# Moving projection pieces so that products on the divided array stand side by side, in a gated DeltaNet and sliding-window attention layer

## The reference

```
h    = rmsnorm(x, pre_norm_w)
proj = h @ w_in                    # q, k, v, gate za (4 heads x 128); b, a (4 + 4); qb, kb, vb, gate zb
# group A: gated DeltaNet
qkv  = silu(causal_depthwise_conv(q, k, v))          # 4 taps
beta = sigmoid(b); g = -exp(a_log) * softplus(a + dt_bias); G = cumsum(g) in a chunk
lower = strict_lower((beta k) k^T * decay)           # 64 x 64 in each chunk
value, k_cum = (I + lower)^-1 [beta v, beta k exp(G)]
o_a  = chunk recurrence over a 128 x 128 state per head
o_a  = rmsnorm(o_a, dn_out_norm_w) * silu(za)
# group B: 8 query heads, 2 key/value heads of 64, a window of two chunks, one sink per head
p    = softmax([rope(qb) rope(kb)^T / 8, sink]) without the sink's column
o_b  = (p vb) * silu(zb)
out  = x + rmsnorm([o_a, o_b] @ w_out, post_norm_w)
```

## Time and profile before

| | |
|---|---|
| median of three runs | 2222.03 us (2221.86 to 2222.96) |
| profiled execution | 2220.89 us, span 2219.1 us |
| one steady step (scores at 1000.99 and 1066.05) | 65.1 us |
| TensorE busy | 94% of the span |
| VectorE / ScalarE / GpSimd busy | 75% / 35% / 31% |
| mean granted TensorE clock | 0.991 of full |
| chain that ended last | TensorE 82%, VectorE 13%, ScalarE 2% |
| DMA | 34 GB/s on average |

### The profile page before, as it was taken

How to read it: one execution, slowest core, us unless ns; L and a number is a source line. 1 busy time by engine, 2 the same in 40 slices (tenths; PEclk the granted TensorE clock), 3 DMA queues, 4 the chain that set the end, 5 groups by cost and what they waited for, 6 DMA issues and landing times.

```text
span 2219.1 us, 63767 instructions
## 1 busy us (share of the span) xinstructions
PE 2089.9 (94%) x26854; PEld 1700.3 (77%) x26854; DVE 1655.8 (75%) x4880; ACT 772.4 (35%) x2200; POOL 688.4 (31%) x1035
## 2 busy tenths in 40 slices
PE   0389999999999999999999999999999999999996
PEld 0378778878878877887887788788788778878874
DVE  5887777777777777777777777777777777777773
ACT  0533333333333333333333333333333333333332
POOL 0023333332323333332333323233322323332332
PEclk9999999999999999999999999999999999999997
DMA  7101000010000100000000000001100000001000
GB/s 296 65 22 32 2 31 32 32 31 32 31 2 31 32 31 32 32 29 4 31 32 31 31 31 17 17 32 32 32 31 31 6 27 32 32 31 32 22 2 29
DMA packets 26335, 75.37 MB, mean 34 GB/s; under 512 B 5129, under 2 KB 9538, under 8 KB 25026
## 3 DMA queue, kind: packets, MB, share of 16 engines
q1 hardware_dynamic: 26050, 71.29, 9.4%
HBM read 54.50 MB, written 16.78 MB: 32 GB/s over the span
## 4 chain that ended last, share of the span: by engine, by line
PE 82%; DVE 13%; ACT 2%; issue 1%; DMA 1%; SPq 0%; POOL 0%; POOLq 0%; DVEq 0%; ACTq 0%
PE bank L406 31%; PE bank L608 15%; PE bank L413 12%; PE bank L421 9%; DVE qkv L896 4%; PE bank L461 2%; PE bank L438 2%; PE bank L576 2%; PE bank L443 1%; PE bank L543 1%; DVE qkv L894 1%; PE bank L564 1%; DVE w_raw L1242 1%; PE bank L384 1%; DVE small L935 1%
## 5 line engine op out<-in xcount | busy, mean ns | idle before, releaser
L406 PE MATMUL bank<-xt_half,w_raw 128*128 128x128 f16 x15360 | 933.0, 219 | 54.5 <-DVE w_raw L1242 53.9
L406 PEld LDWEIGHTS bank<-xt_half,w_raw 128*128 128x128 f16 x15360 | 890.8, 98 | 66.9 <-DVE w_raw L1242 54.1
L896 DVE SCALAR_TENSOR_TENSOR qkv<-conv_in,cols,qkv 128x128 f32<-128x128 f32 x1152 | 436.4, 421 | 3.5
L413 PE MATMUL bank<-w_raw,xt_half 128*128 128x264 f16 (+1 forms) x1536 | 283.7, 328 | 1.0
L1301 POOL TENSOR_TENSOR cw<-mt,small 128x128 f32<-128x128 f32 x320 | 135.1, 446 | 344.7 <-PE bank L438 321.1
L413 PEld LDWEIGHTS bank<-w_raw,xt_half 128*128 128x128 f16 x1536 | 144.3, 99 | 84.3 <-DVE w_raw L911 8.3
L715 ACT ACTIVATE work<-bank 128x128 f32<-128x128 f32 x160 | 44.4, 277 | 372.3 <-PE bank L443 372.3
L608 PE MATMUL bank<-w_o,inv_t 128*128 128x512 f16 x768 | 171.0, 379 | 2.1 <-DVE inv_t L1175 2.1
L608 PE MATMUL bank<-w_o,out_b_half 128*128 128x512 f16 x768 | 171.0, 379 | 0.0
L675 ACT ACTIVATE tanh_c<-qkv 128x512 f32<-128x512 f32 x96 | 60.5, 630 | 281.5 <-DVE qkv L896 281.5
L1349 POOL TENSOR_TENSOR small<-small 128x1 f32<-128x1 f32 x32 | 6.2, 193 | 435.2 <-ACT work L815 435.2
(11 more groups left out here) (215 smaller groups left out, 3575.4 us busy)
## 6 DMA issues: line engine op xcount, KB each, us to landing
x_in<-in_x_dram SPq DMA_DIRECT2D x32, 512.0 KB, 4.7
y_out<-in_x_dram SPq DMA_DIRECT2D x32, 512.0 KB, 4.0
out_dram<-y_out SPq DMA_DIRECT2D x32, 512.0 KB, 2.9
w_raw<-in_w_in_dram SPq DMA_DIRECT2D x8, 1024.0 KB, 13.5
w_o<-in_w_out_dram SPq DMA_DIRECT2D x8, 512.0 KB, 13.4
w_raw<-in_w_in_dram SPq DMA_DIRECT2D x8, 384.0 KB, 12.4
w_raw<-in_w_in_dram SPq DMA_DIRECT2D x8, 256.0 KB, 13.2
rot_tab<-in_rotary_dram SPq DMA_DIRECT2D x32, 64.0 KB, 4.2
```

The costliest lines, as they stand in the source:

```text
L406: last = mm(dst[:, 128 * b:128 * b + 128], w_half[:, c, ws, col:col + 128], xt_half[:, xs, c, :], start=(c == 0 and ws + xs == 0), stop=(c ...
L413: last = mm(dst[:, 0:n_col], xt_half[:, xs, c, :], w_half[:, c, ws, col:col + n_col], start=(c == 0 and ws + xs == 0), stop=(c == NC - 1 a ...
L896: last = v.scalar_tensor_tensor(dst, conv_in[:, b, i:i + TOK], tap, dst, ALU.mult, ALU.add)
```

## The change

Five edits in the step, four on TensorE and one on VectorE:

```diff
                 done(pe, k_win_ready, m)
                 done(pe, at_ready, m)
-                fill(1)
+                fill(2)
...
                 last.then_inc(scores_ready, 1)
-                fill(1)
                 level_p(1)
                 fill(1)
                 level_t(1)
...
                 level_p(3)
+                fill(1)
 
                 done(pe, soft_ready, m)
                 for hh in range(8):
                     last = nc.tensor.transpose(heads(4 + hh // 4)[:, hh % 4, :], soft[:, hh, :], ident)
                 last.then_inc(soft_turned, 1)
                 fill(1)
-                level_t(3)
-                fill(1)
-
                 done(pe, soft_t_ready, m)
                 done(pe, v_win_ready, m)
+                level_t(3)
                 for kv in range(2):
...
+                    couple(1)
                     for half in range(2):
                         last = v.tensor_reduce(row_max[:, 4 * half:4 * half + 4], heads(4 + half), AX_X, ALU.max)
                     last.then_inc(soft_link, 1)
-                    couple(1)
                     dve.wait_ge(soft_link, m * 5 + 1)
```

## The result

The changed kernel takes 2259.99 us (median of four runs, 2258.18 to 2261.03) against 2221.95 for the kernel before (2221.66 to 2222.96). The ratio is 1.017, 95% interval 1.0152 to 1.0187: 38 us slower, where 35 were forecast. The profiled execution took 2258.18 us with a span of 2256.4, 37.3 above the span before.

A forecast was written before the change was run, and what follows sets the result against it. TensorE, busy 94% of the span, was taken as the bound. Per step, waits of 1.23 and 0.29 less 0.41 saved make 1.11 us; 31 steps give 34.4, plus 0.5 for the last: 2257 us, range 2246 to 2270.

The forecast's parts named there:

- The first wait: At the first key/value/gates piece (L413), moved ahead of the scores: TensorE waits 1.23 us a step for VectorE's gate product.
- The second wait: At level 2's first product (L438): TensorE waits 0.29 us a step for VectorE's level update, behind mask and softmax work.
- The reason given for 0.28 instead of 0.48: VectorE's L1066 to L1071 takes 0.28 us, since GpSimd, released by the same product, is done during the reductions.
- The savings: Tiling switches taken away at the scores and around level 3 and the value products: 0.41 us less a step.
- its 0.21: Cost in us of leaving the scores for the next piece, part of it the wait for the gate product L911.
- The seam between the two kinds of tiles: Between level 3's 64*64 product and the 128*64 value products: costs 0.09 us, as much as one to the full array.
- The last step: The mix step without pieces gains at level 1, loses at level 3 waiting for ScalarE's copies; 0.5 us charged.
- Only the first wait: Rival: VectorE gets through the softmax work 0.3 us sooner; 0.82 us a step, 2248 us; chance 0.10.
- hidden: Rival: the gate product comes in time for the moved piece, so not slower; 2218 or 2209 us; chance 0.03.
- the clock falls: Rival: each new wait lowers TensorE's granted clock, 53 us more, 2310 us; chance 0.07.
- More waits: Rival: probabilities' copies and the slower 0.48 add up to 0.4 us a step, to 2269 us; beyond 2264 chance 0.10.
- The wait at L468: At level 6's product, TensorE's 0.3 us wait for VectorE, 31 times: shifts along and gives nothing back.

The follow-up runs named there:

- e1: The changed kernel with the tanh of the gate columns za moved ahead of level 0's four copies on ScalarE; 2221.59 us.
- e3: The changed kernel with the tanh of za ahead of level 0's copies and level 1's mask back behind the two row-maximum reductions; 2212.14 us.
- e5: The kernel before with only the tanh of za moved ahead of level 0's copies on ScalarE; 2219.49 us.
- e4: The kernel before with only the level 3 part: one more piece ahead of the probabilities' transposes, level 3's second product next to the value products; 2220.32 us.

## Why the prediction was right

- *The first wait.* Forecast 1.23, measured 1.23; e1 removes it and it alone. The cause was as read: the kvb piece shares a bank with za, and za's reader starts only behind ScalarE's copies.
- *The second wait.* Forecast 0.29, measured 0.39. Its chain on VectorE was right (mask to L984 3.41 us in the trace, counted from the start of the mask to the end of the update; the sum had 1008.30 - 1004.91 = 3.39). What was mis-sized is when level 2's product is due: level 1's first product, behind the scores, takes 0.23 to its transposes instead of 0.28, so TensorE came 0.05 sooner and waited that much longer for a VectorE that did not come sooner. This half costs the step nothing, as it is also saved ahead of the wait. The other 0.05 does, and is nearly all by which the step outgrew the forecast (1.17 against 1.11): from the start of the first kvb piece to level 2's product it is 1024.24 - 1017.96 = 6.28, forecast 1008.35 - 1002.12 = 6.23. It is made up of links of 0.01 to 0.02 (start of the mask 2.81 behind the piece against 2.79, the 3.41, and 0.06 against 0.05 to TensorE).
- *The reason given for 0.28 instead of 0.48* from L1066 to L1071, that GpSimd would be done by then, fits: 0.28 was measured in the changed kernel, with GpSimd's work of that time over. No run separates GpSimd from whatever else lay beside these two instructions.
- *The savings.* Forecast 0.41. In the changed kernel they are 1.23 + 0.39 - 1.17 = 0.45, with the 0.05 of the shorter first product. Measured as the step of e3 against before, they are 0.40, with 0.08 of waits left in it (0.02 at level 1, 0.06 at level 2). As the forecast said of its 0.21 without giving a size, a part of this is no switch: 0.10 is the old wait for the gate product (e5), so the switches are worth 0.10 + 0.11 + 0.10 = 0.31. The seam between the two kinds of tiles stays, as forecast; e4 shows 0.10 for that part and not 0.2.
- *The sum.* Little of its closeness is luck: of the 0.10 by which the second wait is off, 0.05 is matched by 0.05 more saved, as said. 31 x 1.166 = 36.1 us, and 1.1 us besides, make the 37.3 us of the two spans. The 1.1 are 0.3 ahead of the first mixed step, 0.4 more than 1.17 in that step, 0.2 less in the last step with pieces and 0.6 in the one without. The forecast had 34.4 and 0.5. The median moved by 38.0.
- *The last step.* Of the effects named, both came: level 1's second product waits 0.53 us in place of 1.62, and level 3's second product waits 1.18 us for ScalarE's copies there. A third was not foreseen there: level 2's product waits 2.72 us in place of 1.39, since level 1 is ready early and the update stands behind the reductions.
- *The rivals.* "Only the first wait" is refuted by the 0.39, "hidden" by the 31 waits at L413 (that wait is hidden only where the tanh is moved, e1), "the clock falls" by the window with 1.00. "More waits" did not come in the changed kernel; the transposed probabilities were in time, by 0.15 us (the copies end at 1032.53, the product starts at 1032.68).
- *The wait at L468* shifted along unchanged (0.3 us, 31 times), as forecast.

What stays open is why three of the four runs of the changed kernel lie 1.7 to 2.9 us above its profiled one, at 2258.18.

## What to carry to other kernels

Before a piece of filler work is moved ahead, look up which buffer it writes and who must have read that buffer. Filler that hardly waited may only have been standing late enough. Joining two small-tile sections saves one entry and one exit, here 0.1 us each, so it pays only when no wait of that size is opened. The edits that made it pay were on other engines: an instruction that waited behind unrelated ones in its queue, and an order of two VectorE tasks in which the longer one's input was ready first.

## What the runs showed of the hardware

- Entering 64\*64 work behind full-array work cost 0.10 us, leaving the scores 0.11 (e5). A product of the same kind of tile right behind the scores had no such cost, and ran 0.05 us shorter than behind a piece (0.23 against 0.28).
- Going between 64\*64 and 128\*64 tiles cost about as much as going to the full array (0.28 to the value products in e4, 0.27 to a piece; 0.32 in place of 0.23 for the last block of the value products).
- Waits of 1.2 and 0.4 us in each 66 us did not lower the granted clock (1.00 from 150 to 2190 us).
- Behind the one idle time of 3.37 us near the end the granted clock was 0.66 in the kernel before and 0.50 in e3, and the same sixteen products took 2.74 and 3.58 us.
